# Prompt queries loaded per pair of query blocks, and one sample batch's K pages loaded in an earlier head

## The reference

```
sc = einsum('bqhcd,bkhcd->bhcqk', q, k) * SCALE - slope * dist     # dist < 0 -> -inf
p  = softmax(sc)                    # for each of the two components c
a  = p[:, :, 0] - lam * p[:, :, 1]
o  = einsum('bhqk,bkhv->bqhv', a, v)
```

## Time and profile before

| | us |
|---|---|
| median of 3 runs | 3056.89 (3056.76 to 3059.04) |
| the profiled execution, whole | 3057.13 |
| its span in the profile | 3055.4 |
| TensorE busy | 2957.9 (97% of the span) |
| VectorE busy | 1587.9 (52%) |
| ScalarE busy | 1269.7 (42%) |
| GpSimd busy | 128.2 (4%) |
| prompt attention, about | 2000 to 2659 |
| sample attention, about | 2661 to 2825 |

### The profile page before, as it was taken

How to read it: one execution, slowest core, us unless ns; L and a number is a source line. 1 busy time by engine, 2 the same in 40 slices (tenths; PEclk the granted TensorE clock), 3 DMA queues, 4 the chain that set the end, 5 groups by cost and what they waited for, 6 DMA issues and landing times. The chain is left out here.

```text
span 3055.4 us, 45886 instructions
## 1 busy us (share of the span) xinstructions
PE 2957.9 (97%) x17416; PEld 2486.0 (81%) x17416; DVE 1587.9 (52%) x2678; ACT 1269.7 (42%) x2236; POOL 128.2 (4%) x171
## 2 busy tenths in 40 slices
PE   8999999999989999899999999989999999988898
PEld 7888888889967888788888888869999999855786
DVE  3356555554532111443443433368888888644664
ACT  4444434442221100353433432257777777633322
POOL 0000000000000000000000000010000000021221
PEclk9999999999999999999999999989999999999999
DMA  7433443344344231455555455672444444399452
GB/s 252 154 131 104 144 141 123 115 147 151 115 131 152 89 103 69 155 183 199 190 179 196 158 171 184 176 158 63 102 110 104 104 110 100 125 418 410 147 187 103
DMA packets 272279, 470.06 MB, mean 154 GB/s; under 512 B 23818, under 2 KB 124666, under 8 KB 266074
## 3 DMA queue, kind: packets, MB, share of 16 engines
q1 hardware_dynamic: 270049, 467.47, 47.3%
q0 software_dynamic: 2048, 0.14, 0.0%
HBM read 356.93 MB, written 111.34 MB: 153 GB/s over the span
## 5 line engine op out<-in xcount | busy, mean ns | idle before, releaser
L1756 ACT ACTIVATE attn_scores<-attn_scores,attn_lowest 128x1024 f32<-128x1024 f32 (+15 forms) x256 | 306.8, 1203 | 12.1 <-DVE attn_lowest L1809 12.1
L1809 DVE CUSTOM_DVE_ANT_0 attn_scores<-attn_s,region_early 128x1024 f32<-128x1024 f32 (+7 forms) x256 | 216.8, 856 | 105.4 <-PE attn_s L1697 36.9
L224 PE MATMUL pool_acc<-pool_odd_x_hi,pool_wh 128*128 128x512 f32 (+1 forms) x640 | 223.2, 349 | 0.0
L226 PE MATMUL pool_acc<-pool_odd_x_hi,pool_wl 128*128 128x512 f32 (+1 forms) x640 | 222.9, 348 | 0.0
L225 PE MATMUL pool_acc<-pool_odd_x_lo,pool_wh 128*128 128x512 f32 (+1 forms) x640 | 222.9, 348 | 0.0
L224 PE MATMUL outa_acc<-outa_w_hi,outa_g_hi 128*128 128x512 f32 x512 | 202.3, 395 | 13.9 <-DVE outa_w_lo L1031 9.8
L226 PE MATMUL outa_acc<-outa_w_hi,outa_g_lo 128*128 128x512 f32 x512 | 200.9, 392 | 0.0
L225 PE MATMUL outa_acc<-outa_w_lo,outa_g_hi 128*128 128x512 f32 x512 | 200.8, 392 | 0.0
L224 PE MATMUL pool_acc<-even_x,pool_wh 128*128 128x512 f32 x512 | 200.1, 391 | 0.0
L226 PE MATMUL pool_acc<-even_x,pool_wl 128*128 128x512 f32 x512 | 199.3, 389 | 0.0
L225 PE MATMUL pool_acc<-even_x,pool_wh 128*128 128x512 f32 x512 | 199.2, 389 | 0.0
(11 more groups left out here) (273 smaller groups left out, 6781.6 us busy)
## 6 DMA issues: line engine op xcount, KB each, us to landing
pool_wz<-in_w_in_a SPq DMA_DIRECT2D x18, 2048.0 KB, 8.2
pool_wu<-w_mix SPq DMA_DIRECT2D x16, 2048.0 KB, 8.1
region_early<-in_w_kv SPq DMA_DIRECT2D x16, 2048.0 KB, 9.2
region_early<-in_w_in_b SPq DMA_DIRECT2D x16, 2048.0 KB, 8.7
hold_kq<-in_cache_k SPq DMA_DIRECT2D x64, 512.0 KB, 9.7
region_early<-in_cache_v SPq DMA_DIRECT2D x64, 512.0 KB, 9.5
region_early<-gatedT SPq DMA_DIRECT2D x16, 1024.0 KB, 5.6
gatedT<-pool_gates SPq DMA_DIRECT2D x48, 256.0 KB, 2.2
```

Source lines behind the costliest of these rows:

```text
L224: pe.matmul(out, ah, bh, start=first, stop=False)
L226: return pe.matmul(out, al, bh, start=False, stop=last)
L1756: act.activation(part, part, ACT.Exp, scale=-1.0, bias=low[s][:, x:x + 1], accum_out=sums[s][:, i:i + 1]).then_inc(expd, 1)
L1809: dve.tensor_tensor_reduce(sc[s][:, c, a0:a0 + n], s_ps[idx % 2][:, 0:n], bias[h % 2][:, b0:b0 + n], -SCALE, low[s][:, x - 2:x - 1] if x > ...
```

## The change

In prompt attention the queries are no longer loaded per head. For each unit only its two query blocks are loaded, into one of three small buffers for `qx` and `qs` each, by eight DMAs of 64 KB (two of `qx`/`qs`, two halves of the partitions, two components). K stays per head and both its DMAs are now issued together. The queries of units 0 to 2 are loaded already in the projection stage by `first_loads` of `FirstHead`, those of units 3 and 4 at the start of attention. The space that this frees holds 8 pages (`next`), into which the K pages of sample batch 1 are loaded one by one during head 6 (the seventh). `kp` can so take batch 2's pages right after batch 0's, and `first_loads` of the last layer moves behind V of batch 1, because its weights `w` now lie in `next`, which must be turned first.

```diff
+    def load_queries(self, sp, h, near, far, qx, qs, sem):
+        HD = self.HD
+        for dst, top, bottom in ((qx, "lo", "hi"), (qs, "hi", "lo")):
+            for part, rows in ((top, slice(0, HD)), (bottom, slice(HD, P))):
+                src = self.D[f"qT_{part}"][h * P:(h + 1) * P, :].rearrange("(c p) (n s) -> p c n s", c=2, s=P)
+                for c in range(2):
+                    sp.dma_start(f32(dst[rows, c, :, :]), src[:, c, near:far + 1:far - near, :]).then_inc(sem, 16)
...
+        self.next = m.sb("next", [P, self.NPG, H * P])
...
+            load_q(NQ)
             load_v(0)
-            for n in range(6):
-                load_kq(1, n, slice(0, S), kq_in[1])
+            head0.load_keys(sp, 1, kk[1], k_in[1])
+            load_q(NQ + 1)
             load_v(1)
             nxt.first_rows(sp)
             for u in range(NU):
+                if u >= 2:
+                    sp.wait_ge(scored, (u - 1 + NQ - 2) * NX)
+                    load_q(u + NQ)
                 store(u)
                 h, n = divmod(u + 1, NP)
                 if 1 <= h < H - 1:
                     if n == 0:
                         sp.wait_ge(scored, h * NP * NX)
-                    if n < 6:
-                        load_kq(h + 1, n, slice(0, S), kq_in[(h + 1) % 2])
+                        head0.load_keys(sp, h + 1, kk[(h + 1) % 2], k_in[(h + 1) % 2])
                     elif n == 6:
                         sp.wait_ge(applied, h * NP * NG)
                         load_v(h + 1)
-                elif h == H - 1:
+                if h == H - 2:
                     if n == 0:
                         sp.wait_ge(nxt.tab_in, 16)
+                    nxt.load(sp, "k", 1, n)
+                elif h == H - 1:
+                    if n == 0:
                         sp.wait_ge(scored, h * NP * NX)
...
+                if u >= NQ and x == 0:
+                    pe.wait_ge(q_in[u % NQ], 16 * 8 * (u // NQ))
...
             load_v(0, True)
-            load_k(1)
+            load_k(2)
+            load_v(1)
+            sp.wait_ge(turned, 2 * 2 * NPG)
             last.first_loads(sp)
-            with sp.Fori(2, NB) as b:
+            with sp.Fori(3, NB) as b:
                 load_k(b)
                 load_v(b - 1)
             load_v(NB - 1)
...
             step(0, True)
-            with pe.Fori(1, LB) as b:
+            step(1, False)
+            with pe.Fori(2, LB) as b:
                 step(b, False)
```

More of the change, by code:

```diff
@@ L1467 @@
 class FirstHead:
+    UNITS = 3
     def __init__(self, nc, ctx, D, K, S, tile):
@@ L1473, in __init__, with load_keys @@
         self.kk = tile[:, 0:2 * S].rearrange("p (c s) -> p c s", c=2)
-        self.qx = tile[:, 2 * S:4 * S].rearrange("p (c s) -> p c s", c=2)
+        n = 4 * P
+        q = [tile[:, 2 * S + i * n:2 * S + (i + 1) * n].rearrange("p (c b s) -> p c b s", c=2, b=2) for i in range(2 * self.UNITS)]
+        self.qx, self.qs = q[:self.UNITS], q[self.UNITS:]
         self.sem = self.m.sem("in")
-    def first_loads(self, sp):
[L1478 to L1482, removed]
+    def load_keys(self, sp, h, dst, sem):
+        HD = self.HD
+        for part, rows in (("hi", slice(0, HD)), ("lo", slice(HD, P))):
+            src = self.D[f"kT_{part}"][h * P:(h + 1) * P, :].rearrange("(c p) s -> p c s", c=2)
+            sp.dma_start(f32(dst[rows, :, :]), src).then_inc(sem, 16)
+    def load_queries(self, sp, h, near, far, qx, qs, sem):
+        HD = self.HD
+        for dst, top, bottom in ((qx, "lo", "hi"), (qs, "hi", "lo")):
[3 more added lines that the diff above has]
+                    sp.dma_start(f32(dst[rows, c, :, :]), src[:, c, near:far + 1:far - near, :]).then_inc(sem, 16)
+    def first_loads(self, sp):
+        NB = self.S // P
+        self.load_keys(sp, 0, self.kk, self.sem)
+        for u in range(self.UNITS):
+            near = NB // 2 - 1 - u
+            self.load_queries(sp, 0, near, NB - 1 - near, self.qx[u], self.qs[u], self.sem)
 class FirstPages:
@@ L1494, in __init__ @@
         self.qrow, self.krow = m.sb("q_rows", [R, H * P]), m.sb("k_rows", [R, H * P])
+        KC, N = D["w_out_b"].shape[1] // P, D["w_out_b"].shape[2]
+        with ExitStack() as below:
+            t = Memory(nc, below, "last")
+            self.gh1, self.gl1 = (t.sb(f"{n}1", [P, KC, P], F32R) for n in ("g_hi", "g_lo"))
+            self.y = [t.sb(f"y{i}", [P, N]) for i in range(2)]
+        self.next = m.sb("next", [P, self.NPG, H * P])
+        assert KC * N == self.NPG * H * P
+        self.w = self.next[:, :, :]
+        self.next_in = m.sem("next_in")
         self.tab_in, self.row_in = m.sem("tab_in"), m.sem("row_in")
@@ L1506, in load @@
         n = sp.value_load(self.table[0:1, ds(b * self.NPG + g, 1)], min_val=0, max_val=cache.shape[0] - 1)
-        sp.dma_start(dst[:, g, :], cache[ds(n, 1), :, :, :].rearrange("o p h d -> (o p) (h d)")).then_inc(sem[g], 16)
+        ahead = name == "k" and isinstance(b, int) and b == 1
+        sp.dma_start((self.next if ahead else dst)[:, g, :], cache[ds(n, 1), :, :, :].rearrange("o p h d -> (o p) (h d)")
+                     ).then_inc(self.next_in if ahead else sem[g], 16)
 def attention(nc, D, K, S, H, head0, early, slot, nxt, before):
@@ L1579, in attention @@
         o_ps = [m.ps(f"o{i}", [P, QUAD * P])[:, 0:VD] for i in range(2)]
-        begin_in = m.sem("begin_in")
-        kq_in = [m.sem(f"kq_in{i}") for i in range(2)]
+        k_in = [m.sem(f"k_in{i}") for i in range(2)]
+        q_in = [m.sem(f"q_in{i}") for i in range(NQ)]
         v_sem = [m.sem(f"v_in{i}") for i in range(2)]
@@ L1590, in _, with load_q @@
         def _(sp):
[L1591 to L1598, removed]
+            def load_q(u):
+                if u < NU:
+                    near, far = blocks_of(u)
+                    head0.load_queries(sp, u // NP, near, far, qx[u % NQ], qs[u % NQ], q_in[u % NQ])
             def load_v(h):
@@ L1695, in score @@
                     keys = kk[a][:, c, k0 + o:k0 + o + w]
-                    pe.matmul(out[:, o:o + w], qx[a][:, c, q], keys, start=True, stop=False)
-                    last = pe.matmul(out[:, o:o + w], qs[a][:, c, q], keys, start=False, stop=True)
+                    pe.matmul(out[:, o:o + w], q_low[:, c, r, :], keys, start=True, stop=False)
+                    last = pe.matmul(out[:, o:o + w], q_high[:, c, r, :], keys, start=False, stop=True)
                 last.then_inc(scored, 1)
@@ L1908, in load_k @@
             def load_k(b):
+                before = (b - 2 if isinstance(b, int) and b == 2 else b - 1) * 2 * NPG
                 for g in range(NPG):
-                    sp.wait_ge(turned, (b - 1) * 2 * NPG + 2 * g + 2)
+                    sp.wait_ge(turned, before + 2 * g + 2)
                     first_pages.load(sp, "k", b, g)
@@ L2194, in turn @@
             def turn(b, g, first):
-                pe.wait_ge(k_in[g], 16 * b + 16)
+                ahead = isinstance(b, int) and b == 1
+                if ahead:
+                    pe.wait_ge(first_pages.next_in, 16 * NPG)
+                else:
+                    pe.wait_ge(k_in[g], 16 if first else 16 * b)
+                keys = first_pages.next if ahead else kp
                 for j in range(2):
@@ L2281, with __init__ @@
 class LastLayer:
-    def __init__(self, nc, ctx, D, K, full, rest, H, w_hi, squares):
+    def __init__(self, nc, ctx, D, K, full, rest, H, w_hi, squares, pages):
         self.D, self.K, self.full, self.rest, self.H = D, K, full, rest, H
@@ L2289, in __init__ @@
         m = self.m = Memory(nc, ctx, "last")
[L2290 to L2294, removed]
+        self.gh, self.gl, self.y, self.w = [pages.gh1], [pages.gl1], pages.y, pages.w
         self.gh.insert(0, m.sb("g_hi0", [P, KC, P], F32R))
@@ L2564, in program @@
                 with ExitStack() as above:
-                    final = LastLayer(nc, above, D, K, S // P, R, H, w_hi, slot)
+                    final = LastLayer(nc, above, D, K, S // P, R, H, w_hi, slot, pages)
                     end = sample_attention(nc, D, K, S, H, NB, TS, pages, final, done)
```

25 lines of the change are left out of this document (8 added, 17 removed).

## The result

| | before | after |
|---|---|---|
| median, us | 3057.97 (4 runs, 3056.76 to 3060.45) | 3121.53 (4 runs, 3116.94 to 3123.86) |
| ratio to before, 95% interval | | 1.021 (1.0197 to 1.0222) |
| profiled execution, whole / span | 3057.13 / 3055.4 | 3119.91 / 3118.2 |

The account below looks back on a forecast made before the run. TensorE was taken to bound prompt attention (busy 603.70 of 612 us), the DMA engines sample attention. From 3057.13, 36.6 + 18 + 3.3 + 4.9 = 62.8 us more gave 3120 us, range 3082 to 3145.

Parts of the forecast that it names:

- The time from issue to need: Prompt attention: from T, when SyncE's step begins, TensorE needs the queries loaded in that step 9.3 us later.
- The ordinary unit hidden: Prompt attention, units without K ahead: q lands at T + 7.3 against 9.3, 2.7 us per load as upper bound; cost 0.
- The stall behind K: Fourth unit of heads 1 to 6: q behind 2 MB of K lands 6.1 us late, six times, +36.6 us; head 6's page +1.25.
- the 13 or more that the prediction named as a sign: Prompt attention: q loads behind K should land after 13 us or more, others after under 3.
- the prediction's estimate: Q loads behind K: at 138 GB/s 3.8 us in place of 2.4, 8 us more in total, kept outside the sum.
- The clock: TensorE behind the six K stalls: 3.0 us of work lost at the lower clock each time, +18 us, other end 0.
- The prediction's premise: TensorE's clock stays up after a 3.42 us wait and falls after 3.80 us, so the 6 us waits cost it.
- The smaller late units: Prompt attention: page at K in head 6 +1.25 us, last unit behind four V pages +2.0; together +3.3, ends 0 and 12.
- V's unit: Prompt attention, n = 6: the last q load behind V's 1 MB lands at T + 8.4, just hidden, cost 0.
- Sample attention: Eight pages fewer give -10.0 us, DMA engines idle 14.9 us before V of batch 1: net +4.9, ends +3 and +6.
- Start of attention and projection at 0: Projection stage: 24 small loads take SyncE about 16 us, covered by result buffers; earlier first queries worth nothing; cost 0.
- the 3094 of the terms: Low end of the whole kernel's forecast: 34 us of K stalls, no clock loss, nothing small, +3 in sample attention.

Follow-up runs that it names:

- e7_early_old: Changed kernel with e1_early's edit, no pages in head 6 and sample attention in the order of before; 3056.55 us, ratio 1.0001 to the kernel before.
- e1_early: Changed kernel with each unit's queries issued one unit earlier, still behind K; 3062.25 us, ratio 1.0025 to the kernel before.
- e3_ksplit: Changed kernel with K's two halves issued in two successive steps, each ahead of that step's q loads; 3079.70 us, ratio 1.0080 to the kernel before.
- e11_qfirst_ksplit: Changed kernel with the edits of e2_qfirst and e3_ksplit together; 3063.12 us, ratio 1.0025 to the kernel before.
- e2_qfirst: Changed kernel with the queries issued ahead of K, V and pages in the same step; 3080.13 us, ratio 1.0083 to the kernel before.
- e5_fill: Changed kernel with the row blocks and gain (3.5 MB of the first loads) issued ahead of V of batch 1; 3111.42 us, ratio 1.0178 to before.
- e10_gated: Changed kernel with e1_early's edit, and row blocks, gain and four separately gated weight loads ahead of V of batch 1; 3050.43 us, ratio 0.9981 to before.

## Why the prediction was right

The forecast was 3120 and the measured median is 3121.53; the span of the profiled execution grew by 62.8 us, the same as the sum. The mechanisms forecast are the ones found; the sizes agree less well than the total. Its steps one by one:

- **The time from issue to need**, 9.3 us: right. In the changed kernel it is 9.6 (TensorE would have been ready at 2378.12, the step began at 2368.56).
- **The ordinary unit hidden**: right. Its q loads land in 2.3 to 3.3 us, so the 2.7 was no upper bound, but TensorE never waits there; e7_early_old shows that their number costs nothing.
- **The stall behind K**, six times 6.1 and 1.25 once: 37.9 expected, 36.4 measured. K's second half landed at T + 13.4 (13.0 expected), the last q loads at T + 15.1 (15.4 expected). From their own issue the q loads took 9.1 to 11.5 us, not the 13 or more that the prediction named as a sign; from T it is 12.8 to 15.1. The Trainium skill, page "DMA: Bandwidth & Descriptors", section "Bandwidth", gives 138 GB/s for a transfer of 64 KB, measured on transfers that GpSimd issues; by the prediction's estimate from it each stall would have been 1.4 us longer, and the landing does not bear that out for these loads. e1_early, e3_ksplit and e11_qfirst_ksplit show the cause by taking it away in three ways. What I did not see is that putting the queries first only moves the queueing to the next step.
- **The clock**, six times 3.0: 18 expected, 14.7 measured behind the six long waits, since the low level lasted 3.1 to 6.0 us of work and not 6 each time. A further 1.7 us was lost behind the last short wait, where the prediction had counted none. That 18.1 us were left over against e1_early, so close to 18, is luck. The prediction's premise, that a wait of 3.42 us keeps the clock and a longer one loses it, holds for the waits of 5 us and more, but not for the shorter ones: the clock fell behind the waits of 2.18 us here and 2.21 us in e2_qfirst and not behind the one of 3.12 us there. By the Trainium skill, page "TensorE: Matmul & The Clock Gate", section "Part 1: The HAM clock gate (the "warmup" mystery)", the throttled state is the default and activity releases it; the rows agree, with 0.50 during and behind each long wait and 1.00 after 3.1 to 6.0 us of work.
- **The smaller late units**: 2.0 us expected besides the page at K, 3.5 measured. The wait of 2.18 is the forecast one, at the last unit behind four V pages. V's unit was hidden as forecast except in head 6, where V and a page are both ahead (0.27), which I had called fitting. The wait of 1.02 is at the fourth unit of head 7, behind the first two K pages of batch 0 (issued at 2636.88), a case that the prediction does not name.
- **Sample attention**: the mechanism was right, the size too small. Expected +4.9 with +6 as the end, measured +8.0 up to the last V page and 1.4 given back behind it. The term that was off is the idle time of the DMA engines: the sum over the 5 us stretches from 2735 to 2760 (shares 0.36, 0.02, 0.00, 0.58, 0.89 of 1.03) gives some 16.0 us in place of 14.9, as the share also rises slowly when V's pages start. The remaining 2 us of the 8.0 are not assigned. e5_fill and e10_gated show that the hole is the cause: where it shrinks or goes, the stage is shorter by 9.8 and 17.0 us.
- **Start of attention and projection at 0**: the first reduce comes 1.1 us earlier (2008.23 against 2009.33), small and not tested by itself.

That the total agrees to a microsecond is partly luck: attention came out 1.6 us below its terms and sample attention with the tail 1.7 above, and within attention a clock term that was too high met waits and small losses that the sum did not have. Of the range, the lower end (3082) lies 12 us below the 3094 of the terms without a reason given, and the upper end holds 8 us from the estimate for small transfers, which did not come.

## What to carry to other kernels

When transfers share one queue, a load's lateness is set by the bytes ahead of it, so count for each step, and for the step after it, what is ahead and how long it is until the need; a buffer that is free earlier than it is loaded is time given away, and using it was worth 57 to 59 us here. Taking bytes out of a stage that the DMA engines bound pays only if no gate now leaves their queue empty: look for what had filled the time, and put something there that has no gate or a smaller one. A stall of TensorE costs more than the wait where its clock falls: 14.7 us on top of 36.4 us of long waits here. Read the granted clock of the microseconds behind a wait, since the first product alone does not show it.

## What the runs showed of the hardware that was not expected

- The length of a wait did not decide alone whether TensorE's clock fell. Waits from 5.18 to 7.57 us for q dropped it each time (six in the changed kernel, one in e2_qfirst). Of the shorter ones, 2.18 us (changed kernel) and 2.21 us (e2_qfirst) dropped it for 3.4 us, while 3.12 us (e2_qfirst), 0.5 to 2.33 us (e3_ksplit) and 3.42 us (before) did not. The same wait for ACT in sample attention, 3.50 or 3.51 us, left the clock full in the changed kernel and in e1_early and dropped it in e3_ksplit and e11_qfirst_ksplit, where the 24 transposes behind it took 5.36 us in place of 2.81. The wait in the changed kernel and in e3_ksplit:

```profile
2739.44 2.81 PE L2236 MATMUL smp_t<-all_ident,pages_next 128*128 128x128 f32 x24 [3.50 <-ACT smp_kT L2149]
...
2695.58 5.36 PE L2238 MATMUL smp_t<-all_ident,pages_next 128*128 128x128 f32 x24 [3.51 <-ACT smp_kT L2151]
```

- Two 1 MB loads into the two halves of the partitions, issued 0.64 us apart on one queue, landed 5.4 us apart: 8.0 and 12.8 us after their issue.
- The half megabyte of q behind K took only some 1.7 us beyond K's own landing at 2382.0, less than the 2.4 us by the rate of the 64-partition loads. The first q load landed 11.5 us after 2369.85, some 0.6 us before the K load ahead of it, so landings are not strictly one behind the other.
